# First stage of a hybrid decoder layer: norm squares on two engines, two tiles computed as parts of n appear, dt moved behind them

## The reference

```
n = RMSNorm(h)                       # h: 528 x 1024, mean square over the 1024 columns
[conv_B|conv_C|conv_x|z|xbc|dt_raw] = n @ W_in
xbc  = silu(dwconv4(xbc) + bias)     # 2048 channels, split into x, B, C
dt   = softplus(dt_raw + dt_bias)    # 16 heads
a_cs = cumsum(dt * A) inside each chunk of 128 positions
y    = chunked state-space scan over x*dt, decays exp(a_cs), B, C
h = h + concat(y_conv, y_ssd) @ W_out
h = h + MoE(RMSNorm(h))              # top 4 of 32 experts, clamped SwiGLU
out  = RMSNorm(h)[16:]
```

## Time and profile before

| | us |
|---|---|
| median of 3 runs | 1605.25 |
| the profiled execution's own time | 1617.12 |
| span of the profile | 1615.5 |
| PE busy | 1518.4 (94%) |
| DVE busy | 605.4 (37%) |
| ACT busy | 297.4 (18%) |
| POOL busy | 380.3 (24%) |

### The profile page before, as it was taken

The page is one execution under the profiler, slowest core; times in us unless marked ns, Lnnn a source line. Parts: engine busy times, 40 slices in busy tenths (PEclk is TensorE's granted clock), DMA queues, the critical chain, the costliest instruction groups (busy, mean ns, idle before and its releaser), DMA issues.

```text
span 1615.5 us, 50223 instructions
## 1 busy us (share of the span) xinstructions
PE 1518.4 (94%) x21227; PEld 1282.4 (79%) x21227; DVE 605.4 (37%) x1324; ACT 297.4 (18%) x449; POOL 380.3 (24%) x511
## 2 busy tenths in 40 slices
PE   6898999999995699999999999999999999999994
PEld 4897889875453367799989888889997898999883
DVE  4666988865024222322232222232232223232223
ACT  5442333342021001110110110011011011011102
POOL 1000000000003323233323333232324232333332
PEclk8998999999997799999999999999999999999997
DMA  3222222142446599999999999999999999999983
GB/s 117 78 79 104 105 104 104 56 178 104 197 156 178 202 404 403 398 406 406 406 397 405 404 403 397 403 401 408 402 396 407 405 402 398 407 404 408 395 310 120
DMA packets 88777, 478.79 MB, mean 296 GB/s; under 512 B 16374, under 2 KB 29178, under 8 KB 34610
## 3 DMA queue, kind: packets, MB, share of 16 engines
q1 hardware_dynamic: 65266, 456.94, 70.1%
q0 software_dynamic: 23488, 21.55, 6.7%
HBM read 463.66 MB, written 19.07 MB: 299 GB/s over the span
## 4 chain that ended last, share of the span: by engine, by line
PE 64%; issue 2%; DMA 1%; DVE 1%; POOL 0%; ACT 0%; POOLq 0%; ACTq 0%; DVEq 0%; SPq 0%
PE bank L1399 64%; DMA expert_sum<-moe_f,idx_now 0%; DMA ring<-expert_sum 0%; DMA moe_f<-n_scratch,idx_next 0%; DVE reg_x L1158 0%; DVE reg_b L1146 0%; DVE reg_b L1158 0%; DVE reg_x L1146 0%; POOL slot_table L490 0%; POOL expert_sum L524 0%; DMA idx_raw<-slot_table 0%; POOL idx_raw L504 0%; ACT reg_a L740 0%; DVE moe_f L1095 0%; ACT moe_f L733 0%
## 5 line engine op out<-in xcount | busy, mean ns | idle before, releaser
L1399 PE MATMUL bank<-ring,moe_f 128*32 128x256 f32 x18432 | 1029.9, 380 | 30.6 <-issue 17.4
L1399 PEld LDWEIGHTS bank<-ring,moe_f 128*32 128x32 f32 x18432 | 905.2, 110 | 155.3 <-issue 65.7
L1118 DVE STREAM_TRANSPOSE moe_f<-bank 128x384 f32<-128x384 f32 x64 | 37.3, 583 | 659.1 <-PE bank L1399 635.7
L524 POOL DMA_INDIRECT expert_sum<-moe_f,idx_now x96 | 154.1, 1606 | 341.8 <-ACT moe_f L733 311.4
L1171 PE MATMUL bank<-n_hi,w_hi 128*128 128x264 f32 (+2 forms) x640 | 199.4, 312 | 6.4 <-DVE w_lo L775 5.9
L1171 PE MATMUL bank<-n_lo,w_hi 128*128 128x264 f32 (+2 forms) x640 | 196.5, 307 | 0.0
L1171 PE MATMUL bank<-n_hi,w_lo 128*128 128x264 f32 (+2 forms) x640 | 196.2, 307 | 0.0
L728 ACT ACTIVATE moe_f<-moe_f 128x384 f32<-128x384 f32 x64 | 33.5, 523 | 652.9 <-DVE moe_f L1121 632.1
L1171 PEld LDWEIGHTS bank<-n_hi,w_hi 128*128 128x128 f32 x640 | 121.5, 190 | 15.3 <-issue 8.7
L1171 PEld LDWEIGHTS bank<-n_lo,w_hi 128*128 128x128 f32 x640 | 121.7, 190 | 5.7 <-issue 0.5
L1171 PEld LDWEIGHTS bank<-n_hi,w_lo 128*128 128x128 f32 x640 | 121.6, 190 | 5.5
(11 more groups left out here) (207 smaller groups left out, 848.6 us busy)
## 6 DMA issues: line engine op xcount, KB each, us to landing
ring<-in_moe SPq DMA_DIRECT2D x384, 1024.0 KB, 12.7
ring<-in_w_in SPq DMA_DIRECT2D x24, 1024.0 KB, 5.1
ring<-in_w_out SPq DMA_DIRECT2D x10, 1024.0 KB, 5.6
ring<-acs_scratch SPq DMA_DIRECT2D x4, 1024.0 KB, 6.7
idx_raw<-slot_table POOLq DMA_DIRECT2D x136, 0.8 KB, 5.4
reg_vcs<-in_xT SPq DMA_DIRECT2D x4, 528.0 KB, 6.5
reg_x<-in_xrow SPq DMA_DIRECT2D x4, 512.0 KB, 5.9
expert_sum<-reg_a SPq DMA_DIRECT2D x4, 512.0 KB, 2.8
```

The source lines that it names most:

```text
L524: g.indirect_dma_start(out=acc_parts, in_=y_sb[:, n, :], in_offset=None, out_offset=bass.IndirectOffsetOnAxis(ap=idx_now[:, 2 * n:2 * n + ...
L1118: v.transpose(glu.rearrange("p b (g r) -> p g b r", g=GRANULES), gate).then_inc(gate_raw, 1)
L1399: ins = mm(out[l * LANE:(l + 1) * LANE, g * QUARTER:(g + 1) * QUARTER], x[:, at, g * LANE:(g + 1) * LANE], w[:, l * QUARTER:(l + 1) * QUAR ...
```

## The change

The squares go into eight buffers `sq8`, even slices by ACT, odd ones by DVE. ACT takes a root of a dummy first, and the later root reads PSUM with the scale and eps in the same instruction. ACT casts the first two weight tiles ahead of `n_hi`, and POOL makes their `w_lo`. PE runs seven products of a constant (`warmth`), takes each slice of `n_hi` for tiles 0 and 1 as it appears, then `n_lo`, then dt. dt is laid out on 4 column groups of 32 (one for each chunk of 128 positions; the 16 meta positions are put beside them), so that its chain works on 128 partitions by 144 positions, and its steps stand between the tiles of the first turn, which is written out ahead of the loop.

```diff
 SP
             sp.dma_start(slot(0)[:, 0:KC * 256], win_d[0]).then_inc(w_in[0], 16)
-            sp.dma_start(wdt[:, :], wdt_d).then_inc(par_in, 16)
             sp.dma_start(slot(1)[:, 0:KC * 256], win_d[1]).then_inc(w_in[1], 16)
+            sp.dma_start(wdt, wdt_d).then_inc(par_in, 16)
...
-            sp.wait_ge(acs_ready, 5)
+            sp.wait_ge(acs_ready, 2)
 POOL
-            steps.done(g.memset(pk[:, :], 0.0))
+            steps.done(g.memset(sqb, 1.0))
...
+            for t in range(2):
+                pool.wait_ge(wh_ready, t + 1)
+                g.tensor_tensor(w_lo[:, t, :], slot(t)[:, 0:KC * P], w_hi[:, t, :].bitcast(F32), ALU.subtract
+                                ).then_inc(wl_first, 1)
 ACT
-            for c in range(KC):
-                act.wait_ge(xT_in[c // 2], 16)
-                if c >= 2:
-                    act.wait_ge(sq_used, c - 1)
-                a.activation(sqb[:, c % 2, :], nT[:, c, :], ACT.Square).then_inc(sq_ready, 1)
-            act.wait_ge(free_a, 1)
-            act.wait_ge(free_b, 1)
-            a.activation(t1, t1, ACT.Sqrt).then_inc(rs_root, 1)
-            for c in range(KC):
-                act.wait_ge(norm_ready, c + 1)
-                a.copy(n_hi[:, c, :], nT[:, c, :]).then_inc(nh_ready, 1)
+            act.wait_ge(eps_ready, 1)
+            steps.done(a.activation(small[:, 7:8], eps_col[:, :], ACT.Sqrt))
+            for c in range(0, KC, 2):
+                act.wait_ge(xT_in[c // 2], 16)
+                a.activation(sq8[:, c, :], nT[:, c, :], ACT.Square).then_inc(sqa_ready, 1)
+            act.wait_ge(sq_used, KC)
+            act.sem_inc(free_a, 1)
+            act.sem_inc(free_b, 1)
+            a.activation(t1.rearrange("p (h l) -> p h l", h=2), bank[:, 0:2, 0:HALF], ACT.Sqrt, scale=1.0 / D,
+                         bias=eps_col[:, 0:1]).then_inc(rs_root, 1)
             split(0, None, 0, 0, 16)
             split(1, None, 1, 0, 16)
+            for c in range(KC):
+                act.wait_ge(norm_ready, c + 1)
+                a.copy(n_hi[:, c, :], nT[:, c, :]).then_inc(nh_ready, 1)
...
+            for t in range(A_TILES):
+                take_tile(0, t)          # copies from PSUM, cast of a weight tile
+                if t == 2:
+                    act.wait_ge(par_in, 32)
+                    steps.done(a.activation(a_col[:, :], col("a_log", 0), ACT.Exp))
+                    act.wait_ge(dt_mag, 1)
+                    steps.done(a.activation(da_t, da_t, ACT.Exp))
+                    steps.settled()
+                    a.activation(da_t, da_t, ACT.Ln, bias=1.0).then_inc(dt_e, 1)
+                if t == 3:
+                    act.wait_ge(acs_ready, 2)
+                    for lo, hi in ((0, P), (P, P + META)):
+                        a.activation(wend_t[:, lo:hi], acs_t[:, lo:hi], ACT.Exp, scale=-1.0,
+                                     bias=acs_t[:, hi - 1:hi]).then_inc(wend_e, 1)
+                gated(0, t)              # wait for the convolution, Silu
 DVE
-            dve.wait_ge(sq_used, KC)
-            for hf in range(2):
-                v.tensor_scalar(t1[:, hf * HALF:(hf + 1) * HALF], pair(hf, 0, HALF), 1.0 / D, EPS, ALU.mult, ALU.add
-                                ).then_inc(free[hf], 1)
+            for c in range(1, KC, 2):
+                dve.wait_ge(xT_in[c // 2], 16)
+                v.tensor_tensor(sq8[:, c, :], nT[:, c, :], nT[:, c, :], ALU.mult).then_inc(sqv_ready, 1)
             rooted()
             steps.done(v.reciprocal(t1, t1))
...
-            split(0, 1, 0, 0)
-            split(1, 2, 1, 0)
+            dve.wait_ge(wl_first, 2)
+            dve.sem_inc(wl_ready, 2)
+            split(0, 3, 0, 1)
+            conv_tile(0, 0)
+            conv_tile(0, 1)
+            split(1, 4, 1, 1)
             dve.wait_ge(dt_done, 1)
+            steps.done(v.tensor_scalar(dt_raw_t, bank[:, 4, 0:P + META], col("dt_bias", 0), None, ALU.add))
+            steps.settled()
+            v.scalar_tensor_tensor(da_t, dt_raw_t, -1.0, dt_raw_t, ALU.mult, ALU.min).then_inc(dt_mag, 1)
+            conv_tile(0, 2)
+            split(2, 5, 0, 0)
             dve.wait_ge(dt_e, 1)
...          # dt_t, da_t and two scans instead of five
+            conv_tile(0, 3)
+            split(3, 6, 1, 0)
+            dve.wait_ge(wend_e, 2)
+            v.tensor_tensor(w_t, wend_t, dt_t, ALU.mult).then_inc(pk_ready, 1)
 PE
+            def warmth(n):
+                for _ in range(n):
+                    mm(bank[:, 6, :], warm[:, 0:P], warm, start=True, stop=True)
+            pe.wait_ge(warm_ready, 1)
+            warmth(2)
...          # the squares: 8 slices, 2 matmuls each, as before
+            warmth(5)
+            pe.wait_ge(wh_ready, 2)
+            for c in range(KC):
+                pe.wait_ge(nh_ready, c + 1)
+                part(0, w_hi, n_hi, c, c == 0, False)     # two matmuls, one for each half
+                part(1, w_hi, n_hi, c, c == 0, False)
+                if c == 0:
+                    pe.wait_ge(wl_first, 1)
+                part(0, w_lo, n_hi, c, False, False)
+            for c in range(KC):
+                pe.wait_ge(nl_ready, c + 1)
+                ins = part(0, w_hi, n_lo, c, False, c == KC - 1)
+            ins.then_inc(tile_done, 1)
+            pe.wait_ge(wl_first, 2)
+            for c in range(KC):
+                part(1, w_lo, n_hi, c, False, False)
+                ins = part(1, w_hi, n_lo, c, False, c == KC - 1)
+            ins.then_inc(tile_done, 1)
             pe.wait_ge(par_in, 32)
             for c in range(KC):
-                pe.wait_ge(norm_ready, c + 1)
+                for at, n in ((0, P), (P, META)):
+                    for l in range(LANES):
+                        x = META + l * P if at == 0 else 0
+                        ins = mm(bank[l * LANE:(l + 1) * LANE, 4, at:at + n], wdt[:, c * LANE:(c + 1) * LANE],
+                                 nT[:, c, x:x + n], start=c == 0 and at == 0, stop=c == KC - 1, skip_group_check=True)
+            ins.then_inc(dt_done, 1)
+            a_tile(0, 2)
+            a_tile(0, 3)
+            with pe.Fori(1, A_ITER) as i:
+                for t in range(A_TILES):
+                    a_tile(i, t)
```

More of the change, by code:

```diff
@@ L173, in build @@
         acs_b = view(ring, 5 * PIECE, HEADS, P)
[L175 removed]
+        t1 = view(reg_cs, LEN * KC, LEN)
+        sq8 = view(ring, 2 * PIECE, KC, LEN)
+        warm = view(ring, 5 * PIECE, SEQ)
+        dt_raw_t, dt_t, da_t, acs_t, wend_t, w_t = (view(reg_cs, LEN * (KC + 5) + n * (P + META), P + META)
+                                                    for n in range(6))
         pad_tile = view(reg_cs, LEN * (KC + 4), EXPERTS * CAPACITY * 2 // P).bitcast(I32)
@@ L206, in build @@
         par = sb("par", [P, PAR_W])
-        wdt = sb("wdt", [P, KC * HEADS])
-        dtk = sb("dtk", [P, (TT + 1) * 80])
+        wdt = view(reg_x, 0, KC * LANE)
+        dtk = sb("dtk", [P, 3 * (P + LANE)])
+        eps_col = sb("eps_col", [P, 1])
         dec = sb("dec", [P, HEADS])
@@ L590, in _ @@
             split(1, None, 1, 0, 16)
[L592 to L603, removed]
@@ new lines, in take_tile @@
+            def take_tile(i, t):
+                act.wait_ge(tile_done, i * A_TILES + t + 1)
+                for hf in range(2):
+                    ins = a.copy(stage[:, 3 + hf * HALF:3 + (hf + 1) * HALF], pair(t, hf, HALF))
+                    if hf == 0:
+                        ins.then_inc(staged, 1)
+                    else:
+                        ins.then_inc(free[t % 2], 1)
+                if t < 2:
+                    split(t, None, t, 1)
+                else:
+                    split(t, None, t - 2, 0, i * 16 + 32)
@@ L776, in split @@
                                 w_hi[:, n % 2, :].bitcast(F32), ALU.subtract).then_inc(wl_ready, 1)
-            split(0, 1, 0, 0)
-            split(1, 2, 1, 0)
-            dve.wait_ge(dt_done, 1)
-            dve.wait_ge(norm_ready, KC)
-            for hf in range(2):
-                ins = v.tensor_scalar(t1[0:HEADS, hf * HALF:(hf + 1) * HALF], bank[0:HEADS, 4 + hf, 0:HALF],
-                                      col("dt_bias", 0)[0:HEADS, :], None, ALU.add)
-            steps.done(ins)
+            dve.wait_ge(wl_first, 2)
@@ new lines, in _, with conv_tile @@
+            dve.sem_inc(wl_ready, 2)
+            def conv_tile(i, t):
+                dve.wait_ge(free[t % 2], i * 2 + t // 2 + 2)
+                steps.done(v.tensor_scalar(conv_acc[:, 0:LEN], stage[:, 0:LEN], tap_conv(i * A_TILES + t, 0),
+                                           par[:, ds(i * A_TILES + t + PAR["ssd_bias"], 1)], ALU.mult, ALU.add))
+                for k in range(1, 4):
+                    steps.settled()
+                    ins = v.scalar_tensor_tensor(conv_acc[:, 0:LEN], stage[:, k:k + LEN], tap_conv(i * A_TILES + t, k),
+                                                 conv_acc[:, 0:LEN], ALU.mult, ALU.add)
+                    if k < 3:
+                        steps.done(ins)
```

(9 more changed lines are left out.)

126 lines of the change are left out of this document (54 added, 72 removed).

## The result

The changed kernel takes 1589.37 us (median of 4 runs, 1587.61 to 1590.0) against 1604.84 for the one before (median of 4): a ratio of 0.9899, 95% interval 0.9883 to 0.9915 (the quotient of the two medians is 0.9904, inside it). By the medians it is 15.5 us faster. The forecast was faster by 11.8, at 1593.4; the case without the hold had 14.1.

A forecast was written before the change was run, and what follows sets the result against it. TensorE, busy 94% of the span, bounds the kernel, so only its idle stretches can shrink. Squares 2.1, scaling and table 2.05, hold -1.8, then dt and spread tiles: 11.8 us off 1605.25 gives 1593.4; range 1589.0 to 1599.0.

The forecast's parts named there:

- the case without the hold: Rival at the norm's products: POOL reads beside VectorE without delaying it; tile 6 14.1 us early, 1591.2 us; chance 0.28.
- The squares: Start of the kernel: squares on two engines, no buffer wait, clock up by about 8; end at 13.9, 2.1 us early.
- Scaling and table load: Between squares and reciprocal: DVE's scaling and ACT's table load leave the path, 2.05 us won.
- The hold: At the norm's eight products: POOL's second subtraction delays DVE until 19.9, 1.8 us lost, 2.3 in all; chance 0.42.
- the unheld case: At the norm's products: POOL's subtraction does not delay DVE, products start at 18.17, 1591.2 us; chance 0.28.
- The dip of the clock: TensorE idles 3.1 us before the first n_hi slice; clock at half for some 5 us of work, tile 0 ends 31.4.
- dt on TensorE: Behind tile 1: 64 float32 matmuls take 3.5 us, between 2.0 and 7.2, against 9.72 before; TensorE free at 38.8.
- The chain between the tiles: First turn: dt's steps on ACT and DVE stand between tiles, nearly covered by TensorE's work on tiles 2 to 5.
- The loop's head: Entry to the loop: table load at 55.6, w_lo at 62.3; tile 6 starts there, 64.6 with DVE delayed by POOL.
- the measuring point: Start of tile 6, 76.46 before: everything later is unchanged, so what is won there is won at the end.
- The heavy form of the second: Rival: clock at half until tile 2, TensorE free at 49.6; 10.8 us lost, 1604.2, no change; chance 0.05.
- the third: Rival: clock stays low through tiles 2 and 3, each waiting for w_lo; 20.2 us lost, 1613.7; chance 0.03.

The follow-up runs named there:

- experiment 1: Kernel before plus one Silu on ACT ahead of the loop, so one table load replaces the eight inside it; 1603.45 us, 0.9989 of before.
- experiment 4: Changed kernel without its seven products of a constant; 0.9895 of before.
- experiment 8: Kernel before with the squares in eight buffers and not two, all made by ACT; 0.9998 of before.
- experiment 6: Changed kernel with all eight squares on ACT, none on DVE; 0.9891 of before.
- experiment 3: Changed kernel with POOL's second subtraction given to DVE behind n_lo; for tile 1 TensorE takes n_lo first, w_lo last; 1586.52 us, 0.9883 of before.
- experiment 2: Changed kernel plus an Exp on ACT between the written-out first turn and the loop, bringing back two table loads per turn; 0.9935 of before.
- experiment 7: Changed kernel with the dt chain in one block, ahead of DVE's first convolution and behind the cast of tile 0's turn on ACT; 0.9959 of before.
- experiment 12: Changed kernel run once more, unaltered, beside the variants without the hold; 1588.8 us, 0.9893 of before.

## Why the prediction was right and where it was wrong

The whole was forecast at 11.8 us of gain and came to 15.5. Most mechanisms ahead of tile 6 were right, with these sizes:

- **The squares** were to end at 13.9 and ended at 14.2. The reason given, the clock raised by the first two constant products, is a part of it only: an earlier turn of the durations was worth 0.7 us with the old buffers, and the rest came with the eight buffers, as far as the runs separate the two; the forecast had these as "no wait for a buffer" (experiments 1, 4 and 8). The second engine, which it also counted on, gave 0.1 (experiment 6).
- **Scaling and table load**: forecast 2.05, measured 1.92 (2.85 less 0.93).
- **The hold** was forecast at 1.8 with POOL at 2.0 for one subtraction; it cost 1.95, with POOL at 2.33 for one (4.65 for two). The forecast chose it over the unheld case at 0.42 against 0.28; experiment 3 shows that it was POOL. The rule of the Trainium skill, *SBUF — State Buffer*, on a VectorE instruction with two inputs in SBUF beside a GpSimd one that reads SBUF, which only another form bore out in rows 10, is now borne out for this one: 7.47 us for the eight with POOL beside them, 5.52 without. The estimate of 2.25 from the figure of the Trainium skill, *GPSIMD Engine Reference* (section 3.1), was nearer to the measured 2.33 than my 2.0.
- **The dip of the clock** behind it happened; tile 0 was to end at 31.4 and was copied at 32.8. The clock came back at 28 and not at 26.3. Hold and dip together were to cost 2.3 at tile 0 and cost 3.2 (32.83 against 29.67 in experiment 3). That it falls in such a wait is not certain: with 3.65 or 3.66 us of idle time it fell in four traces (the first, experiments 2, 7 and 12) and not in that of experiment 6.
- **dt on TensorE** was forecast at 3.5 and took 2.44, near the lower end of its range. That made up for the later tiles 0 and 1: tile 2 started at 38.98, against 38.8 forecast.
- **The chain between the tiles** was the main gain, as said (experiment 7). The walk through it put the table load of tile 0's Silu behind the convolution, on the path. It ran in ACT's wait for the convolution, from 34.45, and the Silu followed the convolution at 38.60. TensorE's own work then bounded the copy of tile 2, so this error did not reach tile 6.

The step that failed is this one of the prediction: "The loop's head has a table load (69.66 before), now at 55.6; copy 56.9, convolution 57.8 to 61.1, `w_lo` 62.3, and tile 6 starts there." With it fell the choice of the measuring point: "all that follows hangs on it and is unchanged, so what is won at 76.46 is won at the end." The loads were not the loop's own. ACT entered the loop of the kernel before with the table of Exp, and its end left the table of Silu, so each turn loaded twice. The changed kernel enters it with Silu's table, left by the first turn, and has no load in the loop. This was to be seen in the change: it puts a Silu ahead of the loop where an Exp had stood. The sum then ran so: with the hold the forecast for tile 6 was 64.6, and it was 62.9. The last Silu of the first turn was to end at 57.9 and ended at 57.5, 0.4 of the difference; from there to tile 6 it was 5.4 us and not 6.7, and these 1.3 are the load that is missing. Behind tile 6 came 2.0 more that the forecast had at nothing. Rows 8 show a wait of only 0.16 ahead of tile 6, but with two loads in every turn the copies of tiles 4 and 8 lay 24.2 us apart (70.95 to 95.14) and not 23.4. Experiment 1 takes this gain alone from the old kernel; experiment 2 loses a part of it again in the new one.

Of the rivals, none had this. The heavy form of the second, and the third, never showed: in the thin stretch in which `n_lo` arrives (26 to 30 us without the hold) the clock stayed at 1.00.

What stays open: why experiment 1 gained 3.7 us up to the experts and 1.2 over the whole (its interval reaches to 3.2, which includes the 3.1 of the loads), how the 1.8 us of the squares divide between the early clock and the buffers in the changed kernel, and when exactly an idle TensorE loses its clock.

## What to carry to other kernels

Where an engine's state outlives an instruction, as ACT's table does, look at what the loop is entered with and what its end leaves; if they differ, every turn pays, here 2 x 1.28 us on ACT, of which 0.8 reached the path (24.2 us for a turn and not 23.4). A chain of small steps on two engines costs by where it stands in their queues more than by its own length: the same chain on the same data cost 8.5 us more in one block than between the tiles. And a helper engine's instruction of two operands can hold the main one for nearly its whole length (1.95 of 2.33 us here), so put it beside an instruction that does not compete, as the first of the two subtractions stood beside the reciprocal.

## What the runs showed of the hardware

- A SCALAR_TENSOR_TENSOR of DVE with both tensors in SBUF is held by a POOL TENSOR_TENSOR that reads SBUF: 1.95 us of POOL's 2.33. The RECIPROCAL, with one tensor, was not: 3.45 beside POOL's first subtraction, as before. It had begun 1.0 us ahead of it, and POOL wasn't slowed either (2.33 each).
- 64 float32 matmuls of 32 columns' width, half of them of 128 and half of 16 columns, took 2.44 us on four column groups: 0.038 each.
- After 1.70 us of idle time TensorE's clock was at full in all four traces of the kernels without the hold. After 2.87 (experiment 2) it had fallen, after 3.65 or 3.66 in four traces too, and in that of experiment 6 it had not. Float32 matmuls of 264 columns took 644 ns at a granted 0.50 and 386 at 1.00.
- A table load takes 1.28 us and the next instruction follows at once (57.09, then 58.39 in experiment 2). Exp, Ln, Exp needed a load each (30.43, 37.30 and 39.25 in the kernel before).
